# A two-layer encoder trunk in fp32: 21 taps of the last convolution tile on PE, layer-norm statistics on 32-row blocks, and weight features in runs of 8

## The reference

```python
def conformer_conv(h, w_in, b_in, dw, dw_b, ln_g, ln_b, w_out, b_out):   # layer 0
    u = h @ w_in + b_in
    a, g = jnp.split(u, 2, axis=-1)
    u = a * jax.nn.sigmoid(g)
    u = lax.conv_general_dilated(u, dw[:, None, :], window_strides=(1,),
        padding=[(CONV_WIDTH - 1, 0)], feature_group_count=D_MODEL, ...) + dw_b
    u = jax.nn.silu(layer_norm(u, ln_g, ln_b))
    return u @ w_out + b_out

def hierarchical_moe(...):      # both layers
    ...                         # top-1 of 4 groups, then top-2 of its 8 experts
    return (jax.nn.silu(xr @ w1[e]) * (xr @ w3[e])) @ w2[e]   # weighted, added per token
```

## Time and profile before

| | us |
|---|---|
| median of 3 runs | 1665.13 |
| lowest and highest | 1664.26, 1668.69 |
| the profiled execution | 1667.35 |
| its span, first to last instruction | 1665.6 |
| busy: PE 83%, DVE 28%, ACT 20%, POOL 17% of the span | 1386.0, 459.0, 332.0, 285.9 |
| DMA | 473.64 MB, mean 284 GB/s |
| chain that ended last, by engine | PE 48%, DMA 34%, DVE 8%, POOL 4% |

### The profile page before, as it was taken

The page is one execution under the profiler, slowest core; times in us unless marked ns, Lnnn a source line. Parts: engine busy times, 40 slices in busy tenths (PEclk is TensorE's granted clock), DMA queues, the critical chain, the costliest instruction groups (busy, mean ns, idle before and its releaser), DMA issues.

```text
span 1665.6 us, 16714 instructions
## 1 busy us (share of the span) xinstructions
PE 1386.0 (83%) x5852; PEld 625.3 (38%) x5852; DVE 459.0 (28%) x868; ACT 332.0 (20%) x629; POOL 285.9 (17%) x384
## 2 busy tenths in 40 slices
PE   6995696997888888876699999996998878778783
PEld 3442254332332322322366666544332323223231
DVE  1899514110101101100444444424111011011012
ACT  3555220100000000000434444421100000000000
POOL 3788101111111111110000000001121111111110
PEclk9997796999999999998799999996999999999997
DMA  8222027899999999998600401227899999999994
GB/s 314 79 88 101 0 90 273 347 407 420 420 421 421 420 420 420 417 400 319 249 1 1 152 1 51 102 89 271 334 406 421 420 420 421 419 419 413 417 410 181
DMA packets 91420, 473.64 MB, mean 284 GB/s; under 512 B 19720, under 2 KB 19720, under 8 KB 40432
## 3 DMA queue, kind: packets, MB, share of 16 engines
q1 hardware_dynamic: 78672, 443.64, 65.7%
q0 software_dynamic: 10400, 16.82, 2.7%
q10 hardware_dynamic: 2304, 12.58, 1.9%
HBM read 466.95 MB, written 23.33 MB: 294 GB/s over the span
## 4 chain that ended last, share of the span: by engine, by line
PE 48%; DMA 34%; DVE 8%; POOL 4%; issue 3%; SPq 2%; ACT 2%; ACTq 0%; POOLq 0%; DVEq 0%
DMA ring<-in_moe_w 32%; PE banks L1302 19%; PE banks L1412 5%; PE banks L1248 5%; POOL scratch L526 4%; PE banks L1319 3%; PE banks L1441 3%; SPq L318 2%; PE banks L1193 2%; DVE banks L884 2%; PE banks L1501 2%; PE banks L1456 1%; DMA area<-y_dram 1%; PE banks L1265 1%; PE banks L1483 1%
## 5 line engine op out<-in xcount | busy, mean ns | idle before, releaser
L1302 PE MATMUL banks<-ring,scratch 128*64 128x512 f32 x1984 | 498.4, 653 | 146.6 <-DMA ring<-in_moe_w 134.8
L1302 PEld LDWEIGHTS banks<-ring,scratch 128*64 128x64 f32 x1984 | 158.8, 149 | 482.5 <-issue 482.5
L1028 DVE COPY scratch<-banks 128x256 f32<-128x256 f32 x65 | 27.6, 424 | 801.3 <-PE banks L1310 801.3
L1319 PE MATMUL banks<-ring,scratch 128*64 128x512 f32 x1008 | 230.2, 598 | 3.0 <-DVE scratch L1028 3.0
L696 ACT ACTIVATE scratch<-banks 64x512 f32<-64x512 f32 x65 | 38.2, 588 | 599.2 <-PE banks L1302 599.1
L544 POOL COPY at_out<-rows_out 128x1 int32 (+1 forms) x64 | 11.6, 181 | 700.8 <-ACT scratch L700 700.8
L1412 PE MATMUL banks<-hT,ring 128*128 128x512 f32 x256 | 117.9, 604 | 0.8 <-DVE hT L839 0.8
L1193 PE MATMUL banks<-hT,ring 128*128 128x512 f32 x256 | 113.5, 603 | 3.9 <-DMA ring<-in_conv_w_in 3.9
L526 POOL TENSOR_TENSOR scratch<-scratch 128x512 f32<-128x512 f32 x88 | 111.8, 1271 | 25.2 <-ACT scratch L668 13.2
L1319 PEld LDWEIGHTS banks<-ring,scratch 128*64 128x64 f32 x1008 | 68.1, 136 | 117.3 <-issue 110.3
L1248 PE MATMUL banks<-ring,area 128*128 128x512 f32 x200 | 90.0, 608 | 10.6 <-ACT area L678 9.6
(11 more groups left out here) (208 smaller groups left out, 1146.8 us busy)
## 6 DMA issues: line engine op xcount, KB each, us to landing
ring<-in_moe_w SPq DMA_DIRECT2D x374, 1024.0 KB, 17.2
area<-in_moe_w SPq DMA_DIRECT2D x12, 1024.0 KB, 10.0
ring<-in_attn_w_qkv SPq DMA_DIRECT2D x12, 1024.0 KB, 13.6
ring<-in_conv_w_in SPq DMA_DIRECT2D x8, 1024.0 KB, 10.9
area<-y_dram ACTq DMA_DIRECT2D x8, 1024.0 KB, 7.9
ring<-in_conv_w_out SPq DMA_DIRECT2D x4, 1024.0 KB, 14.4
xn_dram<-area ACTq DMA_DIRECT2D x8, 512.0 KB, 2.6
hT<-in_moe_w SPq DMA_DIRECT2D x4, 1024.0 KB, 6.2
```

What stands on the lines that cost most here:

```text
L1302: last = mm(bank[2 + s][q * SLOTS:(q + 1) * SLOTS, :], xeT[s][:, j, h, :], w[:, c, :], start=c == 0, stop=c == NC - 1)
L1319: last = mm(bank[6 + s][q * SLOTS:(q + 1) * SLOTS, :], hidT[s][:, j, :], w2c[:, j, q * 512:(q + 1) * 512], start=j == 0, stop=j == 3)
```

## The change

Features are laid out as "(p c)": partition p of chunk c is feature 8p + c. A unit is one DMA of 128 partitions (for w1, w3 and w2 with runs of 16 KB), semaphores count 16 per unit, and the normalising copy on ACT writes its columns in the order that keeps `transpose_xn` and the gathers as they were. In the convolution's last tile taps 0 to 20 leave ACT and POOL (and nine of them DVE) and become 21 products on PE of a diagonal matrix with the shifted u; ACT builds the diagonals during tiles 1 to 5. `gated(NC - 1)` moves forward into the taps of the tile before. The statistics are stored as 32 rows per token block, 128 columns wide, so that mean, root and reciprocal work on 128x128; `spread` then makes them 512 wide again in PSUM by products with a column of the identity. The first column half of the output projection goes chunk by chunk over four banks.

```diff
-            v = w[:, c0:c0 + width].rearrange("(h p j) n -> h p j n", h=2, j=4)
-            return [v[h] for h in range(2)]
+            return w[:, c0:c0 + width].rearrange("(p c) n -> p c n", c=NC)
...
-                for h in range(2):
-                    sp.dma_start(dst[h], halves[h]).then_inc(done, 16)
+                sp.dma_start(dst, src).then_inc(done, 16)
...
-                w1v = moe_w1[l].rearrange("e (h p j) n -> e h p (j n)", h=2, j=4)
-                w2v = moe_w2[l].rearrange("e (p h j) n -> e h p (j n)", h=2, j=2)
+                w1v = moe_w1[l].rearrange("e (p c) n -> e p (c n)", c=NC)
+                w2v = moe_w2[l].rearrange("e (p j) n -> e p (j n)", j=4)
...
-                a.activation(xn[:, t, :], x_res[:, t, :], ACT.Copy, scale=rstd[:, t:t + 1]).then_inc(xn_done, 1)
+                a.activation(xn[:, t, :].rearrange("p (h q j) -> p h q j", h=2, j=4),
+                             x_res[:, t, :].rearrange("p (q h j) -> p h q j", h=2, j=4), ACT.Copy,
+                             scale=rstd[:, t:t + 1]).then_inc(xn_done, 1)
...
+            def next_diag():
+                w = diags[0]
+                if w < PE_TAPS:
+                    a.activation(diag[w], ident[:], ACT.Copy, scale=chan[:, NC - 1, w:w + 1]).then_inc(diag_done, 1)
+                diags[0] += 1
...
-                    if w == POOL_TAPS // 2 and ct + 1 < NC:
+                    if w == (POOL_TAPS // 2 if ct < NC - 2 else 4):
                         gate(ct + 1)
-                if ct >= 1:
+                    if 1 <= ct < NC - 2 and w % 2 == 1 and w >= 3:
+                        next_diag()
+                    if ct == NC - 2 and w == 5:
+                        squares(ct - 1)
+                if 1 <= ct < NC - 2:
                     squares(ct - 1)
...
-                for k, w in enumerate(range(POOL_TAPS, TAPS)):
+                taps = range(POOL_TAPS if ct < NC - 1 else PE_TAPS, TAPS)
+                for k, w in enumerate(taps):
...
+                    if ct == NC - 2 and k == 3:
+                        gated(NC - 1)
...
+                else:
+                    link(v.tensor_tensor(uT[:, ct, :], uT[:, ct, :], last, ALU.add))
+                    dve.wait_ge(pe_taps_done, 1)
+                    v.tensor_tensor(uT[:, ct, :], uT[:, ct, :], bank[0][:], ALU.add).then_inc(conv_done, 1)
...
-            link(v.tensor_scalar(ln_mu, bank[4][:], 1.0 / D, None, ALU.mult))
+            link(v.tensor_scalar(ln_mu, bank[4][:, 0:P], 1.0 / D, None, ALU.mult))
...
-                mm(bank[4][:], ones[:], uT[:, ct, :], start=ct == 0, stop=ct == NC - 1)
-                return mm(bank[5][:], ones[:], sq_ct[:, ct, :], start=ct == 0, stop=ct == NC - 1)
+                for dst, src in ((bank[4], uT), (bank[5], sq_ct)):
+                    for t in range(NT):
+                        last = mm(dst[t * ROWS:(t + 1) * ROWS, 0:P], ones[:, 0:ROWS], src[:, ct, t * P:(t + 1) * P],
+                                  start=ct == 0, stop=ct == NC - 1)
+                return last
+
+            def last_taps(lo, hi):
+                if lo == 0:
+                    pe.wait_ge(diag_done, PE_TAPS)
+                    pe.wait_ge(u_done, NC)
+                for w in range(lo, hi):
+                    last = mm(bank[0][:], diag[w], u_buf[(NC - 1) % 2][:, w:w + T], start=w == 0, stop=w == PE_TAPS - 1)
+                return last
+
+            def spread(dst, src):
+
+                for t in range(NT):
+                    last = mm(dst[:, t * P:(t + 1) * P], ident[:, t * ROWS:t * ROWS + 1].to_broadcast([P, P]), src,
+                              start=True, stop=True)
+                return last
...
             stats(NC - 3)
+            last_taps(0, PE_TAPS - 4)
             stats(NC - 2)
+            last_taps(PE_TAPS - 4, PE_TAPS).then_inc(pe_taps_done, 1)
             stats(NC - 1).then_inc(stats_ready, 1)
+            pe.wait_ge(ln_var, 1)
+            spread(mu_wide, ln_mu)
+            pe.wait_ge(ln_rs, 1)
+            spread(r_wide, ln_r).then_inc(ln_wide, 1)
...
+                if l == 0:
+                    for c in range(NC):
+                        pe.wait_ge(ln_done, c + 1)
+                        for t in range(NT):
+                            last = mm(mix_bank(l, t)[:], src[:, c, t * P:(t + 1) * P], w_chunks(n0)[:, c, :],
+                                      start=c == 0, stop=c == NC - 1)
```

More of the change, by code:

```diff
@@ L40 @@
 POOL_TAPS = 12
+PE_TAPS = 21
+ROWS = 32
 HEADS = 8
@@ L221, in trunk @@
         sums = (bank[6], bank[7])
-        ln_mu = area3[:, 1024:1024 + T]
-        ln_r = area3[:, 1024 + T:1024 + 2 * T]
-        ln_t = area3[:, 1024 + 2 * T:1024 + 3 * T]
+        diag = [area3[:, w * P:(w + 1) * P] for w in range(PE_TAPS)]
+        ln_mu, ln_r, ln_t = (area3[:, (PE_TAPS + k) * P:(PE_TAPS + k + 1) * P] for k in range(3))
+        mu_wide, r_wide = bank[6], bank[7]
         xe = [scratch[:, s * 512:(s + 1) * 512] for s in range(2)]
@@ L391, in over_tile @@
                             sp.wait_ge(*freed[k])
[L392 removed]
+                        load_unit(unit(n0 + MOE_UNITS + 3 + k), w, over_w[l] if k < 2 else over_w2[l])
                 with sp.If(n_over > 0):
@@ L519, in _ @@
             k = 0
-            for ct in range(NC):
+            for ct in range(NC - 1):
                 for w in range(1, POOL_TAPS):
@@ L656, in gate @@
                              bias=chan[:, ct, TAPS + 4:TAPS + 5]).then_inc(gate_done, 1)
+            def next_diag():
[3 more added lines that the diff above has]
+                diags[0] += 1
+            diags = [0]
             gate(0)
-            for ct in range(NC):
+            for ct in range(NC - 1):
                 act.wait_ge(u_done, ct + 1)
@@ L885, in _ @@
                     ins.then_inc(dve_taps, 1)
-                tap_count[0] += TAPS - POOL_TAPS
-                if ct + 1 < NC:
+                    if ct == NC - 2 and k == 3:
+                        gated(NC - 1)
+                tap_count[0] += len(taps)
+                if ct + 1 < NC - 1:
                     gated(ct + 1)
                 dve.wait_ge(dve_taps, tap_count[0])
-                dve.wait_ge(tap_added, (ct + 1) * (POOL_TAPS - 1))
-                last = sums[(TAPS - POOL_TAPS) % 2]
@@ L892, in _ @@
-                link(v.tensor_tensor(last, pacc[ct % 2], last, ALU.add))
-                v.tensor_tensor(uT[:, ct, :], uT[:, ct, :], last, ALU.add).then_inc(conv_done, 1)
+                last = sums[len(taps) % 2]
+                if ct < NC - 1:
+                    dve.wait_ge(tap_added, (ct + 1) * (POOL_TAPS - 1))
+                    link(v.tensor_tensor(last, pacc[ct % 2], last, ALU.add))
+                    v.tensor_tensor(uT[:, ct, :], uT[:, ct, :], last, ALU.add).then_inc(conv_done, 1)
+                else:
+                    link(v.tensor_tensor(uT[:, ct, :], uT[:, ct, :], last, ALU.add))
+                    dve.wait_ge(pe_taps_done, 1)
+                    v.tensor_tensor(uT[:, ct, :], uT[:, ct, :], bank[0][:], ALU.add).then_inc(conv_done, 1)
@@ L1237, in mix_out @@
                     loaded(pe, n0 + n)
-                for n in range(2):
+                if l == 0:
[4 more added lines that the diff above has]
+                                      start=c == 0, stop=c == NC - 1)
+                            if c == NC - 1:
+                                last.then_inc(mix_ready, 1)
+                for n in range(1 - l, 2):
                     for t in range(NT):
```

61 lines of the change are left out of this document (29 added, 32 removed).

## The result

| | before | changed |
|---|---|---|
| median, us | 1664.7 (1660.6 to 1668.7) | 1642.7 (1641.6 to 1643.6) |
| ratio, 95% interval | | 0.9871 (0.9845 to 0.9897) |
| profiled execution (span), us | 1667.35 (1665.6) | 1641.64 (1639.5) |

A forecast was written before the change was run, and what follows sets the result against it. It took expert loops to be bound by bandwidth, with a serial path between them. Gains of 6.5 + 0.2 + 2.5 + 1.5 + 8 = 18.7 us gave 1646 us, range 1639 to 1658.

The forecast's parts named there:

- The last tile: Convolution's last tile: with taps moved to PE it ends sooner, gain 6.5 us.
- The sums: Layer norm's sums as eight 32-row products: 1.8 us against 1.98 per tile, gain 0.2 us (0 to 1.2).
- The rival that they run side by side: Layer norm's sums: blocks writing different rows overlap on PE, bringing the total to 1644 us; chance 0.20.
- The normalisation: Layer norm after the convolution: mean, root and reciprocal on 128x128, less the new spreading, gain 2.5 us (2.1 to 3.0).
- The first column half: Output projection: going by channel, PE never waits for ACT, gain 1.5 us (0.6 to 3.1).
- Runs of 8: Expert weight transfers: 16 KB runs raise the plateau's rate, gain 8 us (0 to 14), worked value 9.6.
- packets nothing: Expert weight transfers: bytes alone set the rate, so longer runs gain nothing, result 1654 us; chance 0.20.
- The copies: ACT's normalising copy, now reading runs of 4 floats: expected to cost 0 us more (0 to 9).
- the rival of 1655: ACT's normalising copy: the strided copies cost double, adding 9 us to 1646; chance 0.08.
- the slower rate: Expert weight transfers: 16 KB runs lower the rate, slower than before, 1679 us at 3%; chance 0.06.

The follow-up runs named there:

- warm: Changed kernel with ten idle PE products into an unused bank, ahead of sums, spread and output projection; 1639.7 us, ratio 0.9861.
- by_token: Changed kernel with the first column half of the output projection by token block again; 1642.2 us, ratio 0.9885.
- runs8_only: Kernel before with the new weight layout alone (one 2 MB transfer per unit, 16 KB runs, reordering copy); 1651.3 us, ratio 0.9922.
- after_again: The changed kernel itself, unaltered, measured once more; 1643.5 us, ratio 0.9866.
- warm_late: Changed kernel with three idle PE products, one before the first spread and two before the output projection; 1643.0 us, ratio 0.9868.
- two_dmas: Changed kernel with each weight unit again as two transfers of 8 KB runs, in the new layout; 1654.6 us, ratio 0.9936.

## Why the prediction was right, point by point

The time (1642.7 against 1646, range 1639 to 1658) and the sign hold, and so does what bounds the kernel. The sum of 18.7 stands against 22 by the medians. Term by term:

- **The last tile, 6.5**: 6.0, or 6.7 from the same start. PE released it last, as worked out, but for another reason: seventeen products took 16.15 us, where the prediction had 14.8, the first ones at 1.2 GHz, while the sums of tile 6 took 0.64, where it had 1.8. The two errors cancel (about 1.3 and 1.2), which is luck: the taps ended at 167.3, the prediction had 167.1. The diagonals on ACT (21 of 0.39 us) cost nothing.
- **The sums, 0.2**: this step failed. It priced a 32-row product like a full one, 0.223 us; eight take 0.65 us, so the sums gained 1.3 on the path. The rival that they run side by side came true, with starts 7 ns apart. In kind this is what the Trainium skill (TensorE: Matmul & The Clock Gate, Part 3) states; it has some 4 ns where this trace has 7, and 0.65 us per tile agrees with the "well under 1 us" that the prediction made of it. That different groups of rows are the condition is shown by no run here, since none puts such products into one group. What this rival had missed is its price: PE idle 6.37 us in place of the 1.5 with which the prediction had argued that the clock would hold.
- **The normalisation, 2.5**: 1.7. The narrow operations cost what was said (0.29 us, reciprocal 0.95); the spreads ran at the lower clock, 3.78 us for eight products, 0.47 each and not 0.223. The bound that allowed for it ("doubled if the clock is at its lower level") counted four products; with the clock low the mean's four, ahead of the root's on PE, are no longer hidden whole. So the stretch took 5.1 us where the prediction allowed 3.8 to 4.7; in warm, at full clock, it is 3.9 (169.54 to 173.42).
- **The first column half, 1.5**: 1.6 between the two traces, 1.2 to 1.4 by by_token, and no gap is left between its products. 3.1, its upper bound, is what it gives at full clock (3.2).
- **Runs of 8, 8**: mis-sized, and low. The worked value of 9.6 was nearer than the cautious 8: a run costs 9 ns, not 7.7, which over 25.7 pairs at 0.42 to 0.49 us is 11 to 13. The table of steps has 13.9 in the two stretches with the experts; the trace of runs8_only has 9.9 in the same two, and 13 us by its ratio. Both differences are within what such stretches differ by chance. The forecast of 424 to 426 GB/s and 31.2 us pairs is met. The rival "packets nothing" rested on 431 GB/s in a stretch of 7 us, which was no plateau. The fabric's ceiling of 435 GB/s in the Trainium skill (DMA: Bandwidth & Descriptors, Where 436 GB/s comes from) stays unreached at 426 to 427 in slices of 41.6 us. It lies 3.6% above 420 and 3.1% above the worked 422, so the "under 3%" of the prediction was a little low.
- **The copies, 0**: 1148 ns before and after; the rival of 1655 is out, as is the slower rate.
- **Not in the sum**: 1.7 us between attention's V projection and the first expert product of layer 1. It holds 1.6 us of shorter idle products of PE (four of them, 6.41 us before, 4.85 in the change), an effect of its clock, which was at 0.50 for longer before; it comes and goes from run to run of the same code: in five of the six kernels of the last table that stretch is 330.8 us, in after_again 332.4.

## What to carry to other kernels

Where a queue is bandwidth-bound, price its runs one by one from two plateaus with different run lengths and believe the worked value; the length of the runs showed a price here, the number of transfers none. When products on PE get shorter, look at once at what pause they leave and what clock the products behind it will have, because the gain of one step can be the price of the next. Judge an edit of a few microseconds by a stretch that repeats itself, since in the total it drowns in stretches that differ by three.

## What was not expected of the hardware

- Eight products of 128x32 by 128 columns into four groups of 32 rows take 0.65 us at full clock and 1.08 at the lower one; four of them start 7 ns apart.
- Pauses of 1.5 and 1.3 us with 0.65 us of work between them were followed by products at the lower clock (granted 0.50, 172 to 174 us). With one idle product in the second pause, 0.27 us of it left, the spreads ran at full clock (warm_late, 1.16 us for four).
- A run costs an engine 9 ns beside its bytes, the same from 16 down to 2 KB, with 426, 420, 409 and 387 GB/s, and at 4 KB the same with two transfers a unit and with four.
- Gathers that share the engines land later behind longer packets: 9.1 us with 16 KB, 6.8 with 8 KB (two_dmas), 6.2 with 4 KB, 6.0 with 2 KB.
